# Moving the last modulation gate of layer 0 into routing, with an earlier tail gather and constant matmuls beside routing

## The reference, cut to what matters

```python
mod = silu(cond) @ w_mod[layer] + b_mod[layer]        # 6 * 1024 columns
h   = x + gate1 * mixers(norm(x) * (1 + scale1) + shift1)   # columns 0..3071 (shift1, scale1, gate1)
out = h + gate2 * moe(norm(h) * (1 + scale2) + shift2)      # columns 3072..6143 (shift2, scale2, gate2)
```

## Time and profile before

| | us |
|---|---|
| median of 3 runs | 2015.74 |
| lowest, highest | 2014.8, 2025.67 |
| profiled execution, own time | 2015.61 |
| its span, first to last instruction | 2013.4 |
| PE busy (sum over the span) | 1841.0 |
| DVE busy | 797.9 |
| ACT busy | 566.6 |

### The profile page before, as it was taken

How to read it: one execution, slowest core, us unless ns; L and a number is a source line. 1 busy time by engine, 2 the same in 40 slices (tenths; PEclk the granted TensorE clock), 3 DMA queues, 4 the chain that set the end, 5 groups by cost and what they waited for, 6 DMA issues and landing times.

```text
span 2013.4 us, 36831 instructions
## 1 busy us (share of the span) xinstructions
PE 1841.0 (91%) x15923; PEld 1172.7 (58%) x15923; DVE 797.9 (40%) x1708; ACT 566.6 (28%) x1219; POOL 67.7 (3%) x68
## 2 busy tenths in 40 slices
PE   6999999889889869999998999999899897999974
PEld 2555668667544645555553764468576674555542
DVE  3424456678821541111111552256878324111112
ACT  3113233557610311111110523233567322000000
POOL 0000000000100000000001000000000100000001
PEclk8999999999999969999999999999989996999988
DMA  9821100092251677778988312101000407999993
GB/s 366 312 65 42 32 30 24 22 301 76 84 209 52 228 262 275 293 290 324 388 332 320 118 50 82 32 1 53 22 1 1 169 21 285 345 391 392 394 361 136
DMA packets 165312, 361.40 MB, mean 179 GB/s; under 512 B 11704, under 2 KB 73664, under 8 KB 164896
## 3 DMA queue, kind: packets, MB, share of 16 engines
q1 hardware_dynamic: 142416, 316.30, 42.9%
q0 software_dynamic: 6736, 23.99, 3.7%
q10 hardware_dynamic: 16000, 18.75, 2.6%
HBM read 318.26 MB, written 40.77 MB: 178 GB/s over the span
## 4 chain that ended last, share of the span: by engine, by line
PE 80%; DVE 9%; DMA 5%; ACT 3%; issue 2%; SPq 1%; POOL 0%; POOLq 0%; another core or an unknown queue 0%; ACTq 0%; DVEq 0%
PE ps L1340 16%; PE ps L945 15%; PE ps L1363 8%; PE ps L1227 7%; PE ps L930 6%; PE ps L1055 4%; PE ps L1089 3%; PE ps L1121 2%; PE ps L890 2%; PE ps L1113 2%; PE ps L1399 2%; DMA arena<-in_moe_w_gu 1%; PE ps L1321 1%; DVE att_small L2098 1%; DMA arena<-in_w_mod 1%
## 5 line engine op out<-in xcount | busy, mean ns | idle before, releaser
L1340 PE MATMUL ps<-arena 128*32 128x256 f32 x6080 | 354.0, 386 | 9.9 <-DMA arena<-in_moe_w_gu 8.4
L945 PE MATMUL ps<-arena 128*128 128x256 f32 (+2 forms) x1056 | 349.0, 486 | 0.9 <-ACT arena L1588 0.9
L1340 PEld LDWEIGHTS ps<-arena 128*32 128x32 f32 x6080 | 202.4, 112 | 144.6 <-issue 17.7
L945 PEld LDWEIGHTS ps<-arena 128*128 128x128 f32 x1056 | 198.9, 191 | 130.4 <-issue 116.3
L2504 DVE TENSOR_TENSOR arena<-ps,arena 128x128 f32<-128x128 f32 x95 | 27.7, 292 | 425.7 <-ACT arena L1814 425.7
L1363 PE MATMUL ps<-arena 128*32 128x256 f32 x3040 | 183.3, 382 | 1.3 <-DVE arena L2510 1.3
L1227 PE MATMUL ps<-arena 128*128 128x256 f32 (+1 forms) x512 | 143.4, 434 | 2.0 <-DVE arena L2196 2.0
L1814 ACT ACTIVATE arena<-ps 128x128 f32<-128x128 f32 x95 | 26.3, 277 | 391.1 <-PE ps L1340 391.1
L1055 PE MATMUL ps<-arena 32*128 32x256 f32 (+5 forms) x528 | 132.0, 514 | 3.1 <-ACT arena L1662 2.3
L1713 ACT ACTIVATE arena<-ps,att_small 128x768 f32<-128x768 f32 (+2 forms) x160 | 123.3, 773 | 24.0 <-DVE att_small L2098 22.9
L1363 PEld LDWEIGHTS ps<-arena 128*32 128x32 f32 x3040 | 89.4, 109 | 62.3 <-DVE arena L2510 1.5
(11 more groups left out here) (373 smaller groups left out, 2075.3 us busy)
## 6 DMA issues: line engine op xcount, KB each, us to landing
arena<-in_moe_w_gu SPq DMA_DIRECT2D x32, 4096.0 KB, 20.8
arena<-in_moe_w_down SPq DMA_DIRECT2D x32, 2048.0 KB, 12.9
arena<-in_w_mod SPq DMA_DIRECT2D x24, 2048.0 KB, 18.3
y_rows<-zeros_t SPq DMA_DIRECT2D x2, 9216.0 KB
arena<-in_w_in SPq DMA_DIRECT2D x6, 2048.0 KB, 8.1
arena<-in_w_in SPq DMA_DIRECT2D x8, 1024.0 KB, 5.8
y_rows<-arena ACTq DMA_DIRECT2D x76, 96.0 KB
arena<-in_w_out SPq DMA_DIRECT2D x4, 1536.0 KB, 8.9
```

Source lines behind the costliest of these rows:

```text
L945: last = pe.matmul(PS[:, 4 + k % 2, 0:ch[2]], aT[:, c, t * P:(t + 1) * P], wbuf[:, j % 2, c, 0:ch[2]], start=(c == 0), stop=(c == DC - 1))
L1340: last = pe.matmul(PS[32 * q:32 * q + 32, 2 + g % 2, 0:2 * P], xT(k % 2)[:, a:a + SUB], gate_up_cols(r, c, q), start=(c == 0), stop=(c == ...
```

## The change

1. Jobs are reordered: 0 to 9 are the first ten jobs of layer 0, one beside each of the six chunks of the input projection; 10 to 16 are seven jobs of layer 1 beside the output projection, as before in number; 17 and 18 are the last two of layer 0 (`gate2`), done by PE in routing of layer 0 after the last token tile is copied out, transposed after L1295; 19 to 23 stay in `combine`.
2. SP loads jobs 17 and 18 where the second gate-up buffer lies. The gate-up load of position 1 (4096 KB) therefore moves behind the down loads of positions 0 and 1, and waits for both jobs.
3. `fill_clock`: PE multiplies the constants by the identity into an unused PSUM bank, 3 matmuls of 128x512 before L1295 in both layers, and after it 6 in layer 0 and 3 in layer 1. Their results are not read.
4. `w_mod` is repacked before the launch, so that each run that a DMA reads is 1024 floats, 4 KB.
5. The tail gather waits for one count of `t_pe` less, and for the transposes of the second last block, which free its row buffer.
6. The silu of the third part is computed by ACT before the middle norm; waits on `acol_ready` are renumbered, with a new wait in `experts`.

```diff
-        mod_jobs = [(L, n) for L in range(LAYERS) for n in range(MODN)]
-        MOD_NORM, MOD_NOW, MOD_LATE = 4, 16, 19
+        MOD_NORM, MOD_P, MOD_ROUTE, MOD_LATE = 4, 10, 17, 19
+        mod_jobs = ([(0, n) for n in range(MOD_P)] + [(1, n) for n in range(MOD_ROUTE - MOD_P)]
+                    + [(0, n) for n in range(MOD_P, MODN)] + [(1, n) for n in range(MOD_ROUTE - MOD_P, MODN)])
...
-        MOD_WITH_X = [[4], [5], [6, 7], [8], [9, 10], [11]]
-        MOD_WITH_OUT = {1: 12, 3: 13, 5: 14, 7: 15, 9: 16, 11: 17, 13: 18}
+        MOD_WITH_X = [[4], [5], [6], [7], [8], [9]]
+        MOD_WITH_OUT = {1 + 2 * q: MOD_P + q for q in range(MOD_ROUTE - MOD_P)}
...
-                sp.dma_start(mod_w(i).rearrange("p (k n) -> p k n", k=DC),
-                             io["w_mod"][L].rearrange("(k p) n -> p k n", p=P)[:, :, n * 512:(n + 1) * 512]
+                sp.dma_start(mod_w(i).rearrange("p (a m) -> p a m", a=DC // 2), io["w_mod"][L, n].rearrange("a p m -> p a m")
...
                 if L == 0:
-                    sp.wait_ge(S("wmod_used"), 4 * (MOD_NOW + 1))
+                    sp.wait_ge(S("wmod_used"), 4 * (MOD_ROUTE - 2))
                 load_gate_up(0)
                 if L == 0:
-                    sp.wait_ge(S("wmod_used"), 4 * MOD_LATE)
+                    sp.wait_ge(S("wmod_used"), 4 * (MOD_ROUTE - 1))
+                    mod_load(MOD_ROUTE)
+                    sp.wait_ge(S("op_ps"), STEPS)
+                    mod_load(MOD_ROUTE + 1)
+                    sp.wait_ge(S("wmod_used"), 4 * MOD_ROUTE)
                 sp.wait_ge(S("sq_used"), sq_base(L, 1) + STEPS)
                 load_down(0)
+                if L == 0:
+                    load_down(1)
+                    sp.wait_ge(S("wmod_used"), 4 * MOD_LATE)
                 load_gate_up(1)
-                load_down(1)
+                if L:
+                    load_down(1)
...
+            def fill_clock(n):
+                for _ in range(n):
+                    pe.matmul(PS[:, 7, :], ident, K[:, C_ID:C_ID + 512], start=True, stop=True)
...
+                if L == 0:
+                    pe.wait_ge(S("ftok_a"), OT0[L] + T)
+                    for i in range(MOD_ROUTE, MOD_LATE):
+                        mod_job(i)
+                fill_clock(3)
                 pe.wait_ge(S("oh_ready"), L + 1)
...
                 last.then_inc(S("slot_ps"), 1)
+                if L == 0:
+                    for i in range(MOD_ROUTE, MOD_LATE):
+                        mod_columns(i)
+                fill_clock(3 if L else 6)
...
                 x_transposes(0)
+                if L == 0:
+                    pe.wait_ge(S("acol_ready"), 3)
...
+                if L == 0:
+                    for i in range(MOD_ROUTE, MOD_LATE):
+                        mod_evac(i)
                 dve.wait_ge(S("oh_ready"), L + 1)
                 dve.wait_ge(S("slot_ps"), L + 1)
...
+                    for i in range(MOD_ROUTE, MOD_LATE):
+                        mod_sum(i)
+                    mod_scale(0, 4 * MOD_P, 48, [])
                     dve.wait_ge(S("wtok_ready"), 1)
...
+                pool.wait_ge(S("xt_ps"), I0[L] + NI[L] - 1)
                 lo, n_tail = tail_range(pool, L)
                 with pool.Fori(0, n_tail) as i:
                     o = i + lo
-                    pool.wait_ge(S("t_pe"), 6 * o + (2 * L + 2))
+                    pool.wait_ge(S("t_pe"), 6 * o + (2 * L + 1))
...
+    wm = data["w_mod"].reshape(LAYERS, DC // 2, 2, P, 12, 512)
+    data["w_mod"] = _np.ascontiguousarray(wm.transpose(0, 4, 1, 3, 2, 5)).reshape(LAYERS, 12, DC // 2, P, 1024)
```

More of the change, by code:

```diff
@@ L300, in mod_part @@
         def mod_part(i):
[L301 removed]
+            return 0 if i < MOD_P else 1 if i < MOD_ROUTE else 2
         def mod_banks(i):
[L304 to L308 removed]
+            return (0, 2) if i >= MOD_P else (4, 6)
+        MOD_WITH_X = [[4], [5], [6], [7], [8], [9]]
+        MOD_WITH_OUT = {1 + 2 * q: MOD_P + q for q in range(MOD_ROUTE - MOD_P)}
         OUT_SEGS = [[(0, 512), (512, N)], [(CTX, 512), (512, N)]]
@@ L732, in _ @@
             win_load(0, 1)
-            for i in range(MOD_NORM + 2, MODN):
+            for i in range(MOD_NORM + 2, MOD_P):
                 mod_load(i)
@@ L794, in _ @@
                     sp.wait_ge(S("fin_ps"), 1)
-                    for i in range(MODN, MOD_LATE):
+                    for i in range(MOD_P, MOD_ROUTE):
                         mod_load(i)
@@ L881, in mod_job @@
             def mod_job(i):
-                if i in (0, MODN, MOD_LATE):
+                if i in (0, MOD_P, MOD_ROUTE):
                     pe.wait_ge(S("cc_silu"), mod_part(i) + 1)
@@ L949, in in_proj @@
                         if L == 0 and k == 0:
-                            mod_columns(MODN - 1)
+                            mod_columns(MOD_P - 1)
                         if XB_AT <= k < XB_AT + 2:
@@ L968, in xb_transposes @@
                     pe.wait_ge(S("xbc_ready"), XM * (L + 1))
-                    pe.wait_ge(S("acol_ready"), 2 + 2 * L)
+                    pe.wait_ge(S("acol_ready"), 2 + 3 * L)
                 for t in range(3 * half, 3 * half + 3):
@@ L1232, in out_proj @@
                         i = MOD_WITH_OUT[n]
-                        if i > MODN:
+                        if i > MOD_P:
                             mod_columns(i - 1)
@@ L1236, in out_proj @@
                 if L == 0:
-                    mod_columns(MOD_LATE - 1)
+                    mod_columns(MOD_ROUTE - 1)
                 mid_sums(L, STEPS - 2)
@@ L1520, in tile_norm @@
                     if i:
-                        act.wait_ge(S("acol_ready"), 3)
+                        act.wait_ge(S("acol_ready"), 4)
                         act.wait_ge(S("nrm_x"), nrm_base(1, 0) + i)
@@ L1552, in modulate @@
                     last.then_inc(S("fT_ready"), 1)
-                act.wait_ge(S("acol_ready"), 2 + 2 * L)
+                act.wait_ge(S("acol_ready"), 2 + 3 * L)
                 for n in range(STEPS):
@@ L1874, in _ @@
                     cond_silu(1)
+                    cond_silu(2)
                 mid_norm(L)
                 rows_and_route(L)
-                if L == 0:
-                    cond_silu(2)
                 experts(L)
@@ L1908, in mod_scale @@
                 link(dve.memset(sc[:, 22:23], 0.0))
-                link(dve.tensor_tensor(m, m, bc(bcol3[:, L, j0:j1], (1, j1 - j0), (0, 2)), ALU.add))
+                last = dve.tensor_tensor(m, m, bc(bcol3[:, L, j0:j1], (1, j1 - j0), (0, 2)), ALU.add)
+                if ws:
+                    link(last)
                 for w in ws:
@@ L1962, in conv @@
                 if L == 0:
-                    mod_sum(MODN - 1)
-                    mod_scale(0, 4 * MOD_NORM, 48, [1])
+                    mod_sum(MOD_P - 1)
+                    mod_scale(0, 4 * MOD_NORM, 4 * MOD_P, [1])
             ss3 = ss[:, :].rearrange("p (t h) -> p t h", t=NT)
@@ L2338, in out_proj @@
                     if L == 0 and n in MOD_WITH_OUT:
-                        if MOD_WITH_OUT[n] > MODN:
+                        if MOD_WITH_OUT[n] > MOD_P:
                             mod_sum(MOD_WITH_OUT[n] - 1)
@@ L2348, in out_proj @@
                 if L == 0:
-                    mod_sum(MOD_LATE - 1)
+                    mod_sum(MOD_ROUTE - 1)
                 variance(1)
```

6 lines of the change are left out of this document (2 added, 4 removed).

## The result

The changed kernel takes 2000.24 us (median of four runs, 1996.71 to 2001.47), the kernel before, run beside it, 2017.37 us (four runs). The ratio is 0.9911 [0.9891, 0.9931], so it is faster, by some 17 us. The profiled execution of the changed kernel took 1996.71 us, its span is 1994.8 us; the one before had 2015.61 and 2013.4.

What follows compares the result with a forecast made beforehand. PE was taken to bound the kernel, with 80% of the chain (DMA 5%). The terms -1.5 - 4.6 - 1.0 - 2.0 + 1.2 - 7.5 = -15.4 took 2015.6 to 2000.2 us, range 1992 to 2010.

Steps and rivals of the forecast that it cites:

- Part 1: Start of the kernel: repacked weights load faster, at 415 GB/s instead of 387, -1.5 us.
- Part 2: Input projection: two modulation jobs fewer on PE, 2.29 us each, -4.6 us.
- Part 3: Routing of layer 0: moved jobs hidden under DVE, clock gain -3.4, later first gather +2.4, together -1.0 us.
- near 713: Layer 0 routing: time in us at which the last token tile's copy was expected, against 719.7 before.
- Part 4: Tail of layer 0: earlier gather removes the 1.26 us wait and may speed L1399 by 1.4, taken as -2 us.
- Next in line is PE itself: Tail of layer 0: once the wait for rows goes, PE is the next limit, since the weights are there.
- Part 5: Routing of layer 1: three uncovered fills cost 2.7 us, partly repaid by a higher clock, +1.2 us.
- nearer to no effect: Layer 1 routing: +1.2 us chosen between +2.7 (no clock gain) and -1.8 (full gain), since earlier PE work left the clock low.
- the shift of PE passes on to the end: Layer 1: PE's delay in routing lasts to the end, because gate-up loads wait for PE to free buffers.
- Part 6: Tail of layer 1: earlier gather removes the 6.71 us wait and low-clock time, less 1.3 us for later weights, -7.5 us.
- rival (d): Tail of layer 1 gains nothing because its weights are late; -7.9 us in all, about 2008 us; chance 0.06.
- the bound -5: Tail of layer 1: the smaller gain, -5 us instead of -7.5, if the tail's own weights are late.

Runs made afterwards that it cites:

- e4_nofill: The changed kernel without its fill_clock calls in either layer; 1997.05 us, ratio 0.9957 against the kernel before.
- e7_fill3: The changed kernel with layer 0 fills cut to three behind the row lists and none before them; 1997.66 us, ratio 0.9904 against the kernel before.
- e10_spst: e7_fill3 with the last block's four stores issued by SP instead of ACT, in both layers; 1992.29 us, ratio 0.9894 against the kernel before.
- e3_move: The kernel before with only the two jobs and their loads moved (old weight layout, no fills, late tail gather); 2003.55 us, ratio 0.9969.
- e2_tail: The kernel before with only the earlier gather of the tail rows, in both layers; 2004.41 us, ratio 0.9974.
- e1_repack: The kernel before with only w_mod repacked and its load changed (4 KB runs instead of 2 KB); 2009.44 us, ratio 1.0008.
- e8_halfgu: The changed kernel with half of the tail's gate-up load in layer 1 left out, so it computes something else; one execution, 1996.12 us.
- e6_fills: The kernel before with only the fill_clock calls added, in both layers; 2013.17 us, ratio 0.9986.

## Why the prediction was right, and where it was not

Predicted 2000.2 us, measured 2000.24. That the two agree to 0.04 us is luck. The prediction took 15.4 us off 2015.6; run side by side, the kernel before took 2017.37, so the measured gain is 17.1. And the steps are less good than the sum: two gains were too large, and time at the low clock that fell away in other stages made up for them.

- **Part 1** (-1.5): -2.0 over the kernels, by the traces alone. The rate under 4 KB runs, 408 to 410 GB/s, was near the 415 taken. The fourth load landed 2.4 us earlier, more than that rate explains; why is open. Mechanism right.
- **Part 2** (-4.6): -4.3 for the two jobs. The -6.0 in the profiled pair holds 1.7 us of clock in the first chunk (12.26 before in the earlier trace rows, 10.56 after), which also comes and goes between kernels with the same edits there (10.56 to 13.58).
- **Part 3** (-1.0): -1.2 over the kernels with the early gather (from the last group of logits to the tail), of which e4_nofill gives the moved jobs nothing and the fills all. Right in size, with both of its terms wrong. "I take ... +2.4 for the gather": the gather took 4.3 us. The copies did come as much earlier as forecast (20.2 us behind the last group of logits, which is what "near 713" meant; 19.7 measured). But the two jobs took 3.64 us at full clock, where 720 for their end left some 7. So SP issued the gate-up load of position 1 at 706.08, and it landed 12.5 us later, before the gather went out at 720.04. And of the 4.5 us of clock only 2.6 came (0.7 at L1342, 1.9 at L1361), none of it at the lists: the 5.4 us pause before them let the clock fall. Against that the six fills took 5.98 us instead of the 2.7 counted (the same error as in part 5), past the landing of the rows. e7_fill3 shows the size of that: 2.5 us given away.
- **Part 4** (-2.0): 0 for the wait. The failed step is "Next in line is PE itself". It is ACT, queued behind four store issues; e10_spst takes them away and the step appears (1.4 us). The clock term, 1.7 us in L1422, is there in the profile of the changed kernel, but it comes and goes without regard to the gather (13.97 us in e3_move, 15.67 in e2_tail), so it is not this part's.
- **Part 5** (+1.2): +1.4 in the pair, +1.9 over the kernels, and some +0.7 by the end of the experts. The failed step is "a fill is 0.447 us at full clock (7.13 / 16), so 0.89 at half", which stands in part 3. The row counts products as the trace has them, and each matmul that `fill_clock` issues is two of them: 15 in the program, x30 in the groups by line of the changed kernel. A fill is 0.94 us at full clock and 1.75 at half. The Trainium skill (FP8 and Floating Point Precision, "TensorE Precision Notes") gives true FP32 four passes through the array. If a pass takes a column in a cycle, four times 512 columns are by estimate 0.85 us at 2.4 GHz and 1.71 at 1.2; two products at 0.447 us (0.89) and at 0.87 (1.75) are near that. Three fills came to 3.7 us instead of 2.7, and not to 5.2, because the clock rose among them, which "nearer to no effect" had not expected; it gave back 1.8 at the lists, 0.7 at L1342 and 0.8 at L1361. That "the shift of PE passes on to the end" was wrong for more than half of it.
- **Part 6** (-7.5): -4.7. The failed step is "the queue has run dry, so they land by about 1948.5". The fall of the DMA share at 1947 is where the first of the load's 16 signals came (1947.4); the last came at 1954.0, 22.3 us after the issue. It is 22.0 us in the changed kernel, and 23.5 in e1_repack and e3_move, where the gather is late as before:

```profile
arena<-in_moe_w_gu SPq DMA_DIRECT2D x1, 4096.0 KB, 23.5
```

So the load did not become slower by the change; its lateness was hidden behind the rows. PE's product started at 1960.19, and the weights had lain there for 6.2 us, not for the 11.7 that the sum takes. e2_tail shows the wait for weights with this part alone, e8_halfgu removes it. It is also one of the signs of being wrong that were on record ("L1399 of layer 1 waiting for weights instead of rows"). The text had it as rival (d), in its full form, and named rows 11 against it; a partial form, the bound -5, is what happened.
- **What no step has**: -1.8 us in attention and output projection of layer 0, -3.2 from the tail's down product to layer 1. In the second it is the clock: the first products on the expert rows take 9.74 us before and 8.16 after, the first of layer 1's input projection 8.80 and 7.10. The time at half clock is 2 (1 - g) x span, with g the mean granted clock of the execution: 185 us in the kernel before (0.954), 180 to 181 in e1_repack, e2_tail, e4_nofill and e6_fills, and 144 in e3_move (whose profiled execution has its highest clock) and in both profiles of the changed kernel (0.964). From the down product of layer 0's tail to layer 1 it is 10.2 us before and 3.4 in e1_repack, which changes nothing there. So single stages do change their clock between executions of the same instructions. The whole does not do so by chance: over all executions g is 0.962 to 0.968 in the ten of the changed kernel, and has a median of 0.954 in the 63 of the kernel before in the three groups (one of them reaches 0.962). The medians of the single parts are 0.954 (e1_repack), 0.955 (e2_tail), 0.9585 (e3_move) and 0.959 (e6_fills). The higher clock thus belongs to the changed kernel, and by these medians the moved jobs and the fills bring some half of it each. The prediction has clock terms in the routing stages and the tails alone.
- **Do the parts add up?** By their ratios they give -12.6 us (1.6 + -5.2 + -6.2 + -2.8), by their medians -13.5, by stages about -12. The whole is -17 by its ratio both times, and -17.1 and -14.3 by its medians. The intervals allow for a sum without remainder, so whether the parts gain more together is not settled. The same holds for the gap between e4_nofill and the changed kernel, 9 us by ratios, 2 to 4 by medians and 1.2 by stages.

## What to carry to other kernels

- When a wait goes, list every engine between the released step and the next product, with what its own queue is busy with at that moment: here ACT's store issues and a weight load each stood right behind the row gather, and took back 2 and 3 us of the gains that were counted on.
- A fall of the DMA share is not the landing of the last load: here they lay 7 us apart. Take issue time plus time to landing, if need be from a kernel whose trace has it, and set that against the shifted need.
- Products on constants bought clock here where they ended close to real work: right behind them, but for a pause of 0.85 us, 3.6 us came back (e7_fill3), behind a pause of 3.46 us 1.4 (e6_fills), behind one of 5.40 nothing. More of them than fit in the wait are paid for in full. Before costing a new matmul from a row, check how many products of the trace one matmul of the code makes.
- Compare a forecast with a gain measured side by side, and not with a time: here the base moved by 1.8 us and made the time fit.

## What the runs showed of the hardware

- The clock gained in the fills can be lost in the next pause of PE: in layer 0 the granted clock was 1.00 at 710 to 712 and 0.52 at 712 to 714, with PE idle since 708.7, and in layer 1 the 128 matmuls behind two pauses of 2.18 and 0.77 us took 8.80 us, those behind one of 0.85 us in layer 0 7.11. The Trainium skill (TensorE: Matmul & The Clock Gate, "What's actually happening") says that activity lifts the throttle; no row of the kernel before showed it for fills, and here the rows agree (0.50 in the lists, 0.92 in the fills behind them).
- Four store issues in a row on ACT took 1.8 us, 0.3 to 0.5 us each, during which ACT copies nothing.
- The 16 signals of one 4096 KB load came spread over 6.6 us (1947.4 to 1954.0, the kernel before). The product that needs it waits for the last: in the changed kernel it came at 1941.5 and L1422 started at 1941.63.
- In `combine` DVE started a copy up to 5.6 us after the PE product that it needed had ended (in the changed kernel the product ended 9.7 us after the tail's down product, the copy started at 15.3). Such a delay is in eight of fourteen traces. Why is open.
- The length of stages that no edit touches changed by 1.7 us at a time with the clock at their start, and the ratio of one kernel by 0.4% between two groups on two chips.
